# The two halves of a feed-forward tile in a there-and-back order: first-second in one pass, second-first in the next

## The chip, the cores and the metric

The kernel runs on one core of one Trainium2 chip. The metric is the device time of one execution in microseconds (us), which is that of the one core; it is lower when better.

## The reference, cut to what matters

The reference is a two-layer encoder trunk for one sequence of 512 frames with 16 meta tokens ahead of them, 528 positions in all, at a model width of 1024. Each layer is wrapped by two half-step feed-forward blocks, so there are four of them, and between them stand a convolution and state-space mixer (layer 0) and a sliding-window attention (layer 1). A feed-forward block is

```
h = h + 0.5 * (silu(x @ w_gate) * (x @ w_up)) @ w_down      # x = rmsnorm(h)
# x: 528 x 1024, w_gate and w_up: 1024 x 2816, w_down: 2816 x 1024
```

All is in float32. The meta tokens are dropped in the last layer, so the last feed-forward block has 512 positions only.

## The kernel before

**Tiles and passes.** Activations lie with the features on the 128 partitions and the 528 positions as columns. Each product is made at near float32 accuracy from operands that are split into a high and a low part (`xh` and `xl`, `act_h` and `act_l` for activations, `wh` and `wl` for weights, in a reduced float32 format). A tile of 128 output features is the sum over blocks `k` of 128 input features, and for each block over three passes `q`: `wh` with the high part, `wh` with the low part, `wl` with the high part. Weights are the stationary operand and activations the moving one.

**Two halves, two banks.** A matmul result fits into one bank of PSUM, 512 columns. The 528 positions are therefore taken as two halves of 264 columns, `hf` 0 and 1, each accumulated in a bank of its own: a tile has a pair of neighbouring banks, `ps[:, 2 * pair]` for columns 0 to 263 and `ps[:, 2 * pair + 1]` for columns 264 to 527. Each matmul instruction comes with a weight load of its own, so that a weight block that both halves use is loaded twice. In the last feed-forward block there are 512 columns, one half only (`nb` is 1), and every matmul of a tile writes the same bank.

**The helper.** `mm3` (L795) writes all matmuls of a job, one tile's accumulation, in the order k, q, hf; its matmul instruction is L807. `x_job` calls it for gate and up tiles (8 blocks, so 24 passes a job), and `down` inside `ffn` calls it for down tiles, with 12 blocks in the first part of the feed-forward width and 10 in the second (36 and 30 passes). The first two jobs of the first block have copies of this loop in `first_job` (L864) and `second_job` (L879); the mixer's products are at L1048, L1062 and L1090. All of these alternate the halves too, and the change does not touch them.

**Order of the work.** Each engine has its program written out by hand, and the engines wait for each other by semaphores. TensorE (PE) waits for the split weights (`wl_ready`), for the bank pair to be read out (`tile_evac`), and before a job's last block for the activations (`x_ready`, `act_ready`, in `before_last`). The last matmul of a job raises `tile_full`, for which VectorE (DVE) waits before it reads both halves of the pair in one instruction (L1653 and L1656 for gate and up, L1636 for down). Bank pairs 0 and 1 alternate from job to job. SyncE starts the weight transfers, ScalarE (ACT) makes `wh` (L1309), and DVE makes `wl` (L1591).

**Other matmuls that the prediction speaks of.** The sums of squares (`token_sums`, L817) are plain float32 matmuls of 264 columns, and so are those of the state-space part at L1008 and L1009, of 128 columns. A plain float32 matmul shows as two records in the trace, that is two passes over the same columns of the same bank. L1008 and L1009 add up in the same 128 columns, so four records in a row write the same place.

Of the kernel before, what the change touches and what calls it, by code (L numbers as in the profile page):

```python
# [32 lines left out]
def trunk_program(nc, a, out, stop=None):  # L33
# [56 lines left out]
    with ExitStack() as ctx:  # L90
# [706 lines left out]
        def _(pe):  # L797
            def mm3(pair, slot, blocks, x_h, x_l, k0, col, before_last=None, n_last=1):

                c0, nh, nb = col  # L800
                n = len(blocks)
                for k, b in enumerate(blocks):
                    if k == n - n_last and before_last:
                        before_last()
                    for q, (w, x) in enumerate(((wh, x_h), (wh, x_l), (wl, x_h))):
                        for hf in range(nb):
                            last = nc.tensor.matmul(ps[:, 2 * pair + hf, 0:nh], w[:, slot, b * P:(b + 1) * P],  # L807
                                                    x[:, k0 + k, c0 + hf * nh:c0 + (hf + 1) * nh],
                                                    start=(k == 0 and q == 0), stop=(k == n - 1 and q == 2))
                return last  # L810
# [9 lines left out]
            def x_job(u, j, pair, slot, blocks, col, m=None, new_unit=True):  # L820

                if new_unit:
                    pe.wait_ge(wl_ready, u + 1)
                wait(pe, tile_evac, j - 1)
                before = None
                if m is not None:
                    pe.wait_ge(x_ready, KD * m + KD - 1)
                    before = lambda: pe.wait_ge(x_ready, KD * m + KD)
                mm3(pair, slot, blocks, xh, xl, 0, operand(col), before).then_inc(tile_full, 1)
# [53 lines left out]
            def ffn(n, col):  # L883
# [3 lines left out]
                for part, nf in enumerate(PART):  # L887
# [21 lines left out]
                    def down(i):  # L909
                        for s in range(2):  # L910
                            pe.wait_ge(wl_ready, u0 + s + 2 * i + 1)
                            pe.wait_ge(tile_evac, j0 + s + 2 * i - 1)
                            pe.wait_ge(act_ready[n], done - 1)
                            mm3(s, (u0 + s) % 2, range(nf), act_h, act_l, 0, operand(col),
                                lambda: pe.wait_ge(act_ready[n], done)).then_inc(tile_full, 1)
                            if n == 3 and part == 1 and 2 * i + s:
                                output_tile(2 * i + s - 1)
# [1217 lines left out]
```

## Time and profile before

| | |
|---|---|
| time, median of 3 runs | 1878.01 us (1877.99 to 1879.36) |
| profiled execution, own time | 1878.34 us |
| its span, first to last instruction | 1876.5 us |
| granted TensorE clock, mean over the span | 0.999 |
| PE busy, of the span | 99% (13919 matmuls) |
| weight loads (PEld) busy | 94% (13919 loads) |
| DVE, ACT, POOL busy | 51%, 32%, 19% |

The profile is of one execution. A matmul's end is modelled and matmuls overlap, so a busy share of 99% does not say how fast they follow each other; the distance from start to start does, and the chain of work that ended last gives it as a time for so many matmuls. A granted clock of 1.00 is 2.4 GHz, the upper of the engine's two levels.

### The profile page before, as it was taken

What the parts mean: (1) busy time and instruction counts of PE and PEld (TensorE: products, weight loads), DVE (VectorE), ACT (ScalarE), POOL (GpSimd) and SP (SyncE); (2) the same over time, 40 slices, a digit from 0 to 9 for tenths busy, and PEclk for the clock granted to TensorE, in tenths of its full rate; (3) what the DMA queues carried; (4) which work ended last, traced back from release to release, by engine and by line L of the source; (5) the groups of instructions that cost most, each with busy time, mean ns of one, the idle gap of its engine ahead of it and who ended that gap; (6) DMA issues with size and microseconds to landing.
All of it is one profiled execution on the core that took longest, in us unless ns stands there. A gap on an engine that the chain in (4) does not pass through costs nothing.

```text
span 1876.5 us, 33932 instructions
## 1 busy us (share of the span) xinstructions
PE 1867.1 (99%) x13919; PEld 1767.1 (94%) x13919; DVE 959.9 (51%) x1083; ACT 598.4 (32%) x702; POOL 350.1 (19%) x629
## 2 busy tenths in 40 slices
PE   9999999999999999999999999999999999999999
PEld 8999999999999999999999999999988788888887
DVE  6443356668865443344564443445557654434443
ACT  5222222332243222222342222223456442222232
POOL 2888889315230000000000000000012000000000
PEclk9999999999999999999999999999999999999999
DMA  6322544447423332332243223322321233333322
GB/s 184 90 84 84 155 135 130 162 140 191 118 73 89 94 89 86 110 90 73 71 126 90 84 84 101 90 81 80 115 62 46 66 93 94 90 96 101 111 70 87
DMA packets 330785, 188.29 MB, mean 100 GB/s; under 512 B 8152, under 2 KB 323832, under 8 KB 330712
## 3 DMA queue, kind: packets, MB, share of 16 engines
q1 hardware_dynamic: 323216, 166.71, 30.0%
q0 software_dynamic: 7088, 20.38, 3.9%
q8 instruction: 52, 0.85, 0.2%
q10 hardware_dynamic: 408, 0.17, 0.0%
q14 instruction: 21, 0.17, 0.0%
HBM read 174.91 MB, written 11.14 MB: 99 GB/s over the span
## 4 chain that ended last, share of the span: by engine, by line
PE 96%; DVE 2%; issue 1%; ACT 1%; POOL 0%; POOLq 0%; DVEq 0%
PE ps L807 79%; PE ps L1048 5%; PE ps L1159 2%; PE ps L1090 2%; PE ps L1109 1%; PE ps L1298 1%; PE ps L1260 1%; PE ps L1200 0%; PE ps L1009 0%; PE ps L1008 0%; PE ps L999 0%; DVE r L1621 0%; PE ps L1221 0%; PE ps L1211 0%; ACT xh L1321 0%
## 5 line engine op out<-in xcount | busy, mean ns | idle before, releaser
L807 PE MATMUL ps<-xh,wh 128*128 128x264 f32 (+1 forms) x2432 | 557.7, 299 | 0.3 <-DVE t_a L1653 0.2
L807 PE MATMUL ps<-xh,wl 128*128 128x264 f32 (+1 forms) x2432 | 556.6, 299 | 0.0
L807 PE MATMUL ps<-xl,wh 128*128 128x264 f32 (+1 forms) x2432 | 556.6, 299 | 0.0
L1591 DVE TENSOR_TENSOR wl<-raw,wh 128x2048 fp32r<-128x2048 f32 x171 | 400.2, 2340 | 168.4 <-ACT wh L1309 168.4
L1309 ACT ACTIVATE wh<-raw 128x2048 fp32r<-128x2048 f32 x172 | 327.6, 1905 | 246.4 <-PE ps L807 205.5
L807 PEld LDWEIGHTS ps<-xh,wh 128*128 128x128 f32 x2432 | 385.4, 188 | 15.1 <-issue 1.5
L807 PEld LDWEIGHTS ps<-xl,wh 128*128 128x128 f32 x2432 | 385.2, 188 | 13.8 <-issue 0.2
L807 PEld LDWEIGHTS ps<-xh,wl 128*128 128x128 f32 x2432 | 385.2, 188 | 13.8
L807 PE MATMUL ps<-act_h,wh 128*128 128x264 f32 (+1 forms) x1232 | 282.2, 299 | 0.0
L807 PE MATMUL ps<-act_h,wl 128*128 128x264 f32 (+1 forms) x1232 | 281.7, 299 | 0.0
L807 PE MATMUL ps<-act_l,wh 128*128 128x264 f32 (+1 forms) x1232 | 281.6, 298 | 0.0
L1656 DVE TENSOR_TENSOR t_c<-ps,r 128x528 f32<-128x528 f32 (+1 forms) x88 | 62.0, 704 | 355.3 <-PE ps L807 353.2
L807 PEld LDWEIGHTS ps<-act_h,wl 128*128 128x128 f32 x1232 | 195.2, 188 | 7.0
L807 PEld LDWEIGHTS ps<-act_h,wh 128*128 128x128 f32 x1232 | 195.2, 188 | 6.7
L807 PEld LDWEIGHTS ps<-act_l,wh 128*128 128x128 f32 x1232 | 195.2, 188 | 6.7
L1349 ACT ACTIVATE act_h<-t_c 128x528 f32 (+3 forms) x88 | 56.5, 642 | 446.4 <-DVE t_c L1659 446.4
L332 POOL TENSOR_TENSOR arena<-arena 128x32 f32<-128x32 f32 (+6 forms) x253 | 182.6, 722 | 19.6
L682 POOL TENSOR_SCALAR arena<-arena 128x16 f32<-128x16 f32 x4 | 1.0, 257 | 872.5 <-DVE arena L1992 843.3
L1347 ACT ACTIVATE t_bs<-t_a 128x528 f32<-128x528 f32 (+1 forms) x88 | 56.5, 642 | 276.1 <-DVE t_a L1653 276.1
L1636 DVE SCALAR_TENSOR_TENSOR h<-ps,h 128x528 f32 (+2 forms) x71 | 50.0, 704 | 175.9 <-PE ps L807 168.8
L1661 DVE TENSOR_TENSOR act_l<-t_c,act_h 128x528 f32 (+3 forms) x88 | 65.9, 749 | 78.5 <-ACT act_h L1349 78.5
L1659 DVE TENSOR_TENSOR t_c<-t_c,t_bs 128x528 f32<-128x528 f32 (+1 forms) x88 | 69.5, 790 | 9.0
(313 smaller groups left out, 1685.9 us busy)
## 6 DMA issues: line engine op xcount, KB each, us to landing
raw<-in_ff_w_gate SPq DMA_DIRECT2D x88, 512.0 KB, 3.7
raw<-in_ff_w_up SPq DMA_DIRECT2D x87, 512.0 KB, 4.7
raw<-in_ff_w_down SPq DMA_DIRECT2D x64, 384.0 KB, 3.8
raw<-in_ff_w_down SPq DMA_DIRECT2D x64, 320.0 KB, 3.5
raw<-in_even_w_in SPq DMA_DIRECT2D x16, 512.0 KB, 4.8
raw<-in_attn_w_qkv SPq DMA_DIRECT2D x12, 512.0 KB, 4.5
raw<-in_even_w_out SPq DMA_DIRECT2D x8, 512.0 KB, 4.3
raw<-in_attn_w_o SPq DMA_DIRECT2D x8, 512.0 KB, 4.4
```

What stands on the lines that cost most here:

```text
L332: did(g.tensor_tensor(o, x, y, op))
L807: last = nc.tensor.matmul(ps[:, 2 * pair + hf, 0:nh], w[:, slot, b * P:(b + 1) * P], x[:, k0 + k, c0 + hf * nh:c0 + (hf + 1) * nh], start= ...
L1048: last = nc.tensor.matmul(ps[:, 2 * (p % 2) + hf, 0:L // 2], w[:, slot, b * P:(b + 1) * P], x[:, k, hf * L // 2:(hf + 1) * L // 2], start= ...
L1090: last = nc.tensor.matmul(ps[:, 2 * (d % 2) + hf, 0:L // 2], w[:, slot, b * P:(b + 1) * P], x[:, k, hf * L // 2:(hf + 1) * L // 2], start= ...
L1309: nc.scalar.activation(wh[:, c % 2, :], raw[:, c % 2, :], ACT.Copy).then_inc(wh_ready, 1)
L1347: nc.scalar.activation(t_b[:, cols], t_a[:, cols], ACT.Silu).then_inc(silu_done[n], 1)
L1349: nc.scalar.activation(act_h[:, s + 2 * i, span(operand(col))], t_c[:, cols], ACT.Copy).then_inc(act_h_done[n], 1)
L1591: v.tensor_tensor(wl[:, c % 2, :], raw[:, c % 2, :], wh[:, c % 2, :].bitcast(F32), ALU.subtract).then_inc(wl_ready, 1)
L1636: v.scalar_tensor_tensor(hd, tile(pair, col), scale, hd, ALU.mult, ALU.add).then_inc(tile_evac, 1)
L1656: v.tensor_tensor(halves(t_c, col), tile(1, col), halves(r, col), ALU.mult).then_inc(tile_evac, 1)
L1659: v.tensor_tensor(t_c[:, cols], t_c[:, cols], t_b[:, cols], ALU.mult).then_inc(gated[n], 1)
L1661: v.tensor_tensor(act_l[:, s + 2 * i, span(operand(col))], t_c[:, cols], act_h[:, s + 2 * i, span(operand(col))].bitcast(F32), ALU.subtrac ...
```

## The change

One line in `mm3`. The loop over the halves runs forward in the first pass, backward in the second, forward in the third, and so on through the job: the direction is set by whether `3 * k + q`, the number of the pass, is even. With A for the matmul on columns 0 to 263 and B for that on columns 264 to 527, a job was A B, A B, A B, A B and is now A B, B A, A B, B A. The blocks, passes, weights and waits keep their order, and the order of additions within each half is what it was. Since each job has an even number of passes, each now ends with A. With one half only (`nb` is 1) nothing changes.

```diff
                     for q, (w, x) in enumerate(((wh, x_h), (wh, x_l), (wl, x_h))):
-                        for hf in range(nb):
+                        for hf in range(nb) if (3 * k + q) % 2 == 0 else reversed(range(nb)):
                             last = nc.tensor.matmul(ps[:, 2 * pair + hf, 0:nh], w[:, slot, b * P:(b + 1) * P],
                                                     x[:, k0 + k, c0 + hf * nh:c0 + (hf + 1) * nh],
                                                     start=(k == 0 and q == 0), stop=(k == n - 1 and q == 2))
```

The program of PE, at the end of the last up tile of the first feed-forward block's first part and at the start of its first down tile, in the kernel before. A row is a line, an operation, its tiles and its columns; x2 are the two halves of a pass, and a half that waits for a semaphore stands alone.

```order
L807 MATMUL ps<-xl,wh 128x264 x2
L807 MATMUL ps<-xh,wl 128x264 x2
L904 REGISTER_ALU
L904 COMPARE_AND_BRANCH
L807 MATMUL ps<-act_h,wh 128x264 [waits act_ready0,tile_evac]
L807 MATMUL ps<-act_h,wh 128x264
L807 MATMUL ps<-act_l,wh 128x264 x2
L807 MATMUL ps<-act_h,wl 128x264 x2
```

In the changed kernel these rows read the same, since a row does not tell one half from the other; what moved is inside the x2: in every second one the columns from 264 on come first. The comparison of the two programs on PE, on DVE, which reads the tiles, and on the other three engines:

```order
## PE: 3781 rows in the other, 3781 in this; the same
## DVE: 810 rows in the other, 810 in this; the same
## ACT: 492 rows in the other, 492 in this; the same
## POOL: 381 rows in the other, 381 in this; the same
## SP: 275 rows in the other, 275 in this; the same
```

No instruction is added, taken away, or moved to another pass, and no wait moves.

## Rows read from the trace of the kernel before

**Rows 1.** The page: busy times, granted clock by slices, chain by engine and line.
```profile
PE 1867.1 (99%) x13919; PEld 1767.1 (94%) x13919; DVE 959.9 (51%) x1083; ACT 598.4 (32%) x702; POOL 350.1 (19%) x629
...
PEclk9999999999999999999999999999999999999999
...
PE 96%; DVE 2%; issue 1%; ACT 1%; POOL 0%; POOLq 0%; DVEq 0%
PE ps L807 79%; PE ps L1048 5%; PE ps L1159 2%; PE ps L1090 2%; PE ps L1109 1%; PE ps L1298 1%; PE ps L1260 1%; PE ps L1200 0%; PE ps L1009 0%; PE ps L1008 0%; PE ps L999 0%; DVE r L1621 0%; PE ps L1221 0%; PE ps L1211 0%; ACT xh L1321 0%
```

**Rows 2.** The chain in order of time: start us, length us, what; longest pieces.
```profile
41.16 357.12 PE ps L807 x2976
...
589.87 374.65 PE ps L807 x3120
...
971.21 368.89 PE ps L807 x3072
...
1520.65 307.65 PE ps L807 x1356
```

**Rows 3.** Groups of PE by line and shape: count, busy us, mean ns, idle before.
```profile
L807 PE MATMUL ps<-xh,wh 128*128 128x264 f32 x2080 | 420.1, 283 | 0.1
...
L807 PE MATMUL ps<-act_h,wh 128*128 128x264 f32 x1056 | 213.0, 283 | 0.0
...
L807 PE MATMUL ps<-xh,wh 128*128 128x512 f32 x352 | 137.6, 391 | 0.2 <-DVE t_a L1653 0.2
```

**Rows 4.** Stretches, instructions of L807 alone: busy us, granted clock, DMA share.
```profile
620.00:740.00 120.00, 120.00 (x1002) 120.00 (x1002) 1.00 0.29 86
1180.00:1300.00 120.00, 120.00 (x1003) 120.00 (x1002) 1.00 0.27 80
1720.00:1810.00 90.00, 90.00 (x399) 74.59 (x398) 1.00 0.29 85
```

**Rows 5.** Timeline near 156 us, up tile to down tile: start us, length us.
```profile
155.72 0.40 PE L807 MATMUL ps<-xl,wh 128*128 128x264 f32 x2
155.84 0.31 PEld L807 LDWEIGHTS ps<-xh,wl 128*128 128x128 f32 x2
155.96 0.40 PE L807 MATMUL ps<-xh,wl 128*128 128x264 f32 x2
156.09 0.31 PEld L807 LDWEIGHTS ps<-act_h,wh 128*128 128x128 f32 x2
...
156.20 0.40 PE L807 MATMUL ps<-act_h,wh 128*128 128x264 f32 x2
...
156.40 0.71 DVE L1656 TENSOR_TENSOR t_c<-ps,r 128x528 f32<-128x528 f32 x1 [4.45 <-PE ps L807]
156.44 0.40 PE L807 MATMUL ps<-act_l,wh 128*128 128x264 f32 x2
```

**Rows 6.** Timeline of PE near 1640 us, last block, one half of 512 columns.
```profile
1639.74 0.39 PE L807 MATMUL ps<-xh,wh 128*128 128x512 f32 x1
1639.97 0.39 PE L807 MATMUL ps<-xl,wh 128*128 128x512 f32 x1
1640.19 0.39 PE L807 MATMUL ps<-xh,wl 128*128 128x512 f32 x1
1640.42 0.39 PE L807 MATMUL ps<-act_h,wh 128*128 128x512 f32 x1
1640.65 0.39 PE L807 MATMUL ps<-act_l,wh 128*128 128x512 f32 x1
```

**Rows 7.** Timeline of PE near 438 us, plain float32 passes of 128 columns.
```profile
438.07 0.38 PE L1008 MATMUL ps<-arena 128*66 128x128 f32 x2
438.29 0.38 PE L1009 MATMUL ps<-arena 128*66 128x128 f32 x2
...
439.82 0.38 PE L1008 MATMUL ps<-arena 128*66 128x128 f32 x2
```

**Rows 8.** Timeline of PE near 404 us, plain float32 passes of 264 columns.
```profile
403.88 1.05 PE L817 MATMUL ps<-ssq,ones 128*128 128x264 f32 x4
404.58 0.60 PE L1048 MATMUL ps<-xh,wh 128*128 128x264 f32 x2
405.01 0.40 PE L1048 MATMUL ps<-xl,wh 128*128 128x264 f32 x2
```

**Rows 9.** What PE waited for at L807: us in total, times, longest.
```profile
PE ps L807 <- DVE t_a L1653: 0.2, 1, 0.2
```

## The prediction

> **What bounds the kernel now.** I read the page first. The chain that ended last is 96% TensorE, and 79% of the span is the one matmul line that the change edits; the clock stands at its upper level in every slice [rows 1]. Next I looked for waits that the new order could fill or lengthen, and there are none: at L807 TensorE waited 0.2 us in the whole run [rows 9]. So the kernel's time is a count of matmuls times the distance from one start to the next, and this distance is the only thing that the change can move.
>
> The chain in order of time gives it. In the blocks with two halves, 3120 matmuls take 374.65 us, 120.1 ns each, and 3072 take 368.89 us, also 120.1; the first block has 2976 in 357.12 us, 120.0. In the last block, with 512 columns, 1356 take 307.65 us, 226.9 ns each [rows 2]. The stretches say the same (1002 in 120 us), with the clock at 1.00 and the weight loads busy without a gap where the matmuls have 264 columns, but only 74.59 of 90 us where they have 512 [rows 4]. The timeline shows the beat: a pass of two halves every 0.24 us, straight across the end of a tile (155.72, 155.96, 156.20, 156.44), with VectorE reading the finished pair behind it [rows 5].
>
> **The change part by part.** *What is removed, added and moved.* Nothing but the order of the two halves in every second pass. The count of matmuls and of loads stays, and so do all waits: the wait ahead of a job's last block stands before whichever half comes first, and the signal that the tile is full stays on the job's last matmul, when both halves are complete as before. VectorE reads both halves in one instruction, which starts some 0.4 us after the start of the last pass [rows 5]; which half was last is nothing to it. Weight loads do not get fewer: the two halves of a pass have the same weights now, and yet there are 13919 loads for 13919 matmuls [rows 1]. Four in a row with the same `wh` (first and second pass) exist already, and each is loaded. This part of the edit costs nothing, and it needs no cover, since nothing is issued more.
>
> *What differs physically.* Before, every matmul in a tile wrote another bank than the one ahead of it. Now the second matmul of a pass and the first of the next write the same bank, and the same columns of it. How many such places: 2080 matmuls of `xh` and `wh` at 16 a job are 130 gate and up jobs, of 24 passes; 1056 of `act_h` and `wh` are 48 down jobs [rows 3]. All passes together are 1.5 times 3136, so 4704. Less one for each of the 178 jobs, whose end still changes the pair, 4526 places turn from a change of bank into a repeat. With a cost of c ns at each, the time moves by 4.526 us per ns.
>
> *The price c.* No row before shows a repeat with 264 columns of this format, so I bound it from rows nearby.
>
> From above, by the last block. There every matmul repeats its bank within a tile. If a column takes a cycle at 2.4 GHz, as plain passes at two cycles a column suggest (below), 512 columns take 213.3 ns and 264 take 110.0; what is left is 13.6 ns with the bank repeated and 10.1 ns with the bank changed. If the whole difference were the price of repeating, c would be 3.5 ns. That is the upper end: 15.8 us.
>
> From the other side, a change of bank could be what costs, so that c is negative. Of the 10.1 ns that remain with 264 columns, plain passes keep some 2 to 3 (below); the rest, 7 ns at most, would go at each repeat: 31.7 us gained. But the form with no change of bank has the larger remainder, not the smaller.
>
> In the middle, the plain float32 passes. At L1008 and L1009 four records in a row write the same 128 columns of one bank, and from 438.07 to 439.82 us there are 16 records, 109.4 ns each [rows 7]. At L817 two records go to one bank and two to the next; from 403.88 to 405.01 stand these four and one pass of 0.24 us, so 0.89 us for four, 222.5 ns each [rows 8]. The difference is 113.1 ns for 136 columns, 0.83 ns or two cycles a column, and the remainder is 2.7 ns with all repeats (109.4 less 106.7) and 2.5 ns with half of them changes of bank (222.5 less 220.0). Repeating costs no more than changing here, although the same place is written again after 109 ns, sooner than the 120 ns of the changed order. The last block agrees as far as its times are given: from the last up tile to the first down tile the bank changes, and the starts are 0.23 us apart there (1640.19, 1640.42) as between the repeats around it (0.23, 0.22) [rows 6]; at 10 ns a step this excludes a large price, not 3.5 ns.
>
> I take c as zero, by the plain passes, which are nearest to the question asked (a repeat of the same columns after about the same time), while the 3.5 ns rest on two widths that may differ for another reason, for example a cost that grows with the columns.
>
> *The sum.* The profiled execution takes 1878.34 us, of which 1876.5 are span. Plus 4526 times 0 ns this stays 1878.3, and in terms of the median, which lies 0.3 us lower, 1878.0. What a measurement of this kernel can tell from no change is about 0.2%, 3.8 us, or c of 0.83 ns.
>
> **The rivals.** *Repeats cost (slower).* The accumulating write to a bank would have to let the write ahead of it finish, at the pass boundaries of L807. Price up to 3.5 ns at 4526 places, so up to 1893.8 us; from 0.83 ns on it decides. For it: the larger remainder of the 512-column form. Against it: rows 7. The order also makes the moving operand jump back, where second halves used to follow their first halves in memory; if that costs, it has the same sign and place, and I count it here.
>
> *Changes of bank cost (faster).* Then 4526 of them vanish, at up to 7 ns: down to 1846.6 us. For it: the 10.1 ns that no row explains. Against it: the 512-column form and L817, which gain nothing where the bank repeats. The Trainium skill has a rule of this kind (TensorE: Matmul & The Clock Gate, section "A second HAM failure mode: psum-queue depth-cycling"): cycling through PSUM banks at each iteration lets the engine idle so often that its clock is cut back and restored by turns. By that rule fewer changes of bank would speed this kernel up; but the trace shows no cut to undo, since the granted clock is 1.00 in the very stretches that alternate banks at each matmul [rows 4].
>
> *Loads bound it, so no order matters (no change).* Where matmuls have 264 columns, loads lie end to end or over each other for all of 240 us [rows 4]. If it is they that set the beat, a small c would hide behind them: 1878.0 again. This is the forecast by another road. Against it: a transfer that is always under way need not be the one that is waited for.
>
> **How the numbers follow.** No change: 0.76, with a range of its own of 1874.3 to 1881.8. Slower by a repeat's cost: 0.13, spread from 1881.8 to 1893.8. Faster: 0.11, spread from 1846.6 to 1874.3, most of it near the upper end, since all of the 7 ns can hardly go. The range from 1873 to 1888 holds the first case, half of the second and a little of the third, some 0.83 together; the upper end is c of 2.2 ns, beyond the middle of its bounds. The chances by 0.2% are those of the cases.
>
> **What would show it.** If I am right, the chain has pieces of L807 with the same 120.0 to 120.1 ns each (3120 in 374 to 375.4 us), passes 0.24 us apart, weight loads without gaps, and 226.9 ns in the last block. If repeats cost, the 264-column pieces grow, at 3.5 ns to 121.8 ns a matmul (380 us for 3120), and weight loads show gaps at pass boundaries, while the last block stays at 307.65 us. If changes of bank cost, the same pieces shrink. A change in the clock, or a wait of TensorE at L807 above a few us, would mean that something moved which I hold fixed. The prediction is wrong if the start-to-start distance depends on which half went before, which no row of before can show.

## The result, and the profile after

The changed kernel takes 1884.10 us (median of 5 runs, 1881.80 to 1887.51) against 1878.21 us before: a ratio of 1.0031, with a 95% interval of 1.0017 to 1.0045. It is slower by 5.9 us. The forecast was 1878.0 us and no change; the time lies inside the stated range (1873 to 1888), on the side of the rival that I gave 0.13. Measured once more beside the experiments, the same program took 1889.41 us (1884.70 to 1892.58) against 1878.56, a ratio of 1.0057 (1.0044 to 1.0070). So its times scatter over more than 10 us, where those of the kernel before stay within 4. One execution of the kernel before (2235.17 us) and one of the second-first run below (3087.40 us) stand far apart from all others and enter no ratio and no scatter given here.

The page of the changed kernel, its lines that answer to [rows 1]: busy times and the granted clock by slices.

```profile
span 1882.1 us, 33932 instructions
...
PE 1872.2 (99%) x13919; PEld 1771.6 (94%) x13919; DVE 960.1 (51%) x1083; ACT 598.3 (32%) x702; POOL 350.7 (19%) x629
...
PEclk9999999999999999999999999999999999999999
```

Counts, clock and the other engines are as before. The chain in order of time (start us, length us, what), against [rows 2]:

```profile
40.80 280.34 PE ps L807 x2304
...
333.48 70.35 PE ps L807 x576
...
595.43 374.65 PE ps L807 x3120
...
976.77 368.88 PE ps L807 x3072
...
1526.25 307.65 PE ps L807 x1356
```

Read it from the end. The last block has 307.65 us for 1356, to the digit what it had; the second and third blocks have 374.65 and 368.88 us, also the old numbers within 0.01. The first block is the one that changed: 280.34 us for 2304 are 121.7 ns each, where it had 120.0. It begins at 40.80 us (before 41.16) and the next piece after it, the first matmul of the mixer, stands at 403.83 us, where it stood at 41.16 plus 357.12, so at 398.28. The first block is 5.9 us longer, and that is the whole loss: 2976 matmuls times 1.67 ns are 5.0 us, and what TensorE waited at L807, against [rows 9], is another 0.7:

```profile
PE ps L807 <- DVE t_a L1653: 0.9, 2, 0.7
```

Counts of matmuls in a stretch of each of the three blocks with two halves show the pace best (stretch us, its length, PE busy and count, granted clock, DMA share, GB/s). A stretch counts the two matmuls at its edges too, so the pace is the length over the count less two.

```profile
100.00:280.00 180.00, 180.00 (x1482) 1.00 0.37 114
640.00:880.00 240.00, 240.00 (x2002) 1.00 0.31 90
1020.00:1260.00 240.00, 240.00 (x2002) 1.00 0.31 92
```

At 120.0 ns a stretch of 180 us would have 1502, and one of 240 us 2002. The first block has 1482: 121.6 ns, with TensorE busy throughout and the clock at 1.00. In the timeline of the first block (start us, length us) ten starts of passes show it as 2.19 us for nine passes, 0.243 us each, where [rows 5] have 0.24:

```profile
99.77 0.41 PE L807 MATMUL ps<-xh,wh 128*128 128x264 f32 x2
100.01 0.41 PE L807 MATMUL ps<-xl,wh 128*128 128x264 f32 x2
...
101.72 0.40 PE L807 MATMUL ps<-xh,wl 128*128 128x264 f32 x2
101.96 0.28 PE L807 MATMUL ps<-xh,wh 128*128 128x264 f32 x1
```

So one program runs the same loop at two paces, and keeps one for hundreds of microseconds. It does not even begin the block at the longer one. Ahead of the long piece the chain has the block's first two jobs at L807, and then other matmuls:

```profile
28.02 11.52 PE ps L807 x96
...
39.78 1.02 PE ps L977 x8
```

96 matmuls in 11.52 us are 120.0 ns each; the longer pace starts behind the break. The starts in the kept trace, read to the nanosecond, show what it is made of. From 100 to 150 us the distances come round every 12 matmuls (125, 124, 123, 118, 125, 121, 120, 124, 120, 116, 124, 120; together 1460 ns, 121.67 each), from 640 to 700 us every four (119, 121, 120, 120). In the longer pace the distances are 120.5 ns on the mean at the boundary of two passes, where a half is repeated, and 122.8 inside a pass: the added time does not stand at the repeat.

### The profile page after: what moved, and what is told of

It is laid out like the page before. It is cut to its first block, busy times and chain, and to the rows that moved or that the text cites. A ratio compares the mean times of both kernels' runs of the same rounds, so it can differ in the third digit from the quotient of the medians.

```text
span 1882.1 us, 33932 instructions
## 1 busy us (share of the span) xinstructions
PE 1872.2 (99%) x13919; PEld 1771.6 (94%) x13919; DVE 960.1 (51%) x1083; ACT 598.3 (32%) x702; POOL 350.7 (19%) x629
## 4 chain that ended last, share of the span: by engine, by line
PE 95%; DVE 2%; issue 1%; ACT 1%; DMA 0%; POOL 0%; SPq 0%; ACTq 0%; DVEq 0%
PE ps L807 78%; PE ps L1048 5%; PE ps L1159 2%; PE ps L1090 2%; PE ps L1109 1%; PE ps L1298 1%; PE ps L1260 1%; PE ps L1200 0%; DMA raw<-in_ff_w_gate 0%; PE ps L1009 0%; PE ps L1008 0%; PE ps L999 0%; DVE r L1621 0%; PE ps L1221 0%; PE ps L879 0%
## 5 line engine op out<-in xcount | busy, mean ns | idle before, releaser
L807 PE MATMUL ps<-xh,wh 128*128 128x264 f32 (+1 forms) x2432 | 558.5, 299 | 0.9 <-DVE t_a L1653 0.9
L807 PE MATMUL ps<-xl,wh 128*128 128x264 f32 (+1 forms) x2432 | 557.0, 299 | 0.0
L807 PE MATMUL ps<-xh,wl 128*128 128x264 f32 (+1 forms) x2432 | 555.7, 298 | 0.0
L807 PEld LDWEIGHTS ps<-xh,wh 128*128 128x128 f32 x2432 | 385.7, 188 | 16.0 <-issue 1.4
L807 PEld LDWEIGHTS ps<-xh,wl 128*128 128x128 f32 x2432 | 386.5, 188 | 13.9
L807 PEld LDWEIGHTS ps<-xl,wh 128*128 128x128 f32 x2432 | 386.6, 188 | 13.8 <-issue 0.2
L807 PE MATMUL ps<-act_h,wh 128*128 128x264 f32 (+1 forms) x1232 | 282.5, 299 | 0.0
L807 PE MATMUL ps<-act_l,wh 128*128 128x264 f32 (+1 forms) x1232 | 281.8, 299 | 0.0
L807 PE MATMUL ps<-act_h,wl 128*128 128x264 f32 (+1 forms) x1232 | 281.2, 298 | 0.0
L807 PEld LDWEIGHTS ps<-act_h,wl 128*128 128x128 f32 x1232 | 195.8, 188 | 7.1
L807 PEld LDWEIGHTS ps<-act_l,wh 128*128 128x128 f32 x1232 | 195.8, 188 | 6.6
L807 PEld LDWEIGHTS ps<-act_h,wh 128*128 128x128 f32 x1232 | 195.3, 188 | 6.8
L332 POOL TENSOR_TENSOR arena<-arena 128x32 f32<-128x32 f32 (+6 forms) x253 | 192.4, 760 | 19.6
```

The lines of the kernel that those rows point to most:

```text
L332: did(g.tensor_tensor(o, x, y, op))
```

## The experiments

All are timed beside the kernel before on the same chip. In what follows A is the matmul on columns 0 to 263, B that on 264 to 527. "Pace" is that of the three stretches above, in ns a matmul. The diffs of banks and columns alone are against the changed kernel; the others hold for the kernel before, or for the changed kernel where the order A B B A is named. Where a diff sets `at`, the moving columns are read from `at` on; that line is left out in the last ones.

### The changed kernel again

> The changed kernel once more, as the measure for the others on the same chip. In its profile above, the first block ran at 121.7 ns a matmul and the second and third at 120.1. Theory S (a block falls into one of two states at its start and keeps it; in the one state the new order costs 1.67 ns a matmul, in the other nothing): times scatter from about 1878 to 1893.5 us in steps of some 5 us a block (3000 matmuls times 1.67 ns), and each block of the profile is either at 120.0 to 120.1 or at about 121.7 ns. Rival F (a fixed cost of the first block, say of its transfers): 1884 us in every run within 1 us, first block slow, the other two not.

1889.41 us (1884.70 to 1892.58), 1.0057 (1.0044 to 1.0070). Stretches in this profile, and the chain around the start of its second block:

```profile
100.00:280.00 180.00, 180.00 (x1482) 1.00 0.37 114
640.00:880.00 240.00, 240.00 (x2003) 1.00 0.31 91
1020.00:1260.00 240.00, 240.00 (x2002) 1.00 0.31 92
```
```profile
583.71 5.84 PE ps L807 x48
589.55 0.89 PE ps L817 x4
590.44 21.64 PE ps L807 x178
```

Again the first block is at 121.6 and the others are at 120.0, but the second block began at the other pace: its first job took 5.84 us for 48 (121.7 ns; before the change 5.76 to 5.77). By 640 us it ran at 120.0. In between, the stream was broken by the sums of squares (L817) at 589.55 us, and by a gap at 596.24 us, where the timeline has a pass that begins 0.36 us after the one ahead of it. So a block does not keep the pace that it begins with, as theory S had it. The scatter fits the rest of theory S: one block at the longer pace costs about 5.2 us, two 10.4, three 15.6, so that 1884, 1889 and 1893 are such sums. The profiled executions agree: 1884.10 and 1884.70 us with one long block, 1889.20 with two (columns alone, below). Some times (1887.5, 1881.8) lie between, as they would if a block changed its pace on the way; none of these has a trace. Rival F, a fixed cost of the first block, falls by the scatter and by the run with turned columns alone, below.

### The banks alone, and the columns alone

```diff
-for hf in range(nb) if (3 * k + q) % 2 == 0 else reversed(range(nb)):
-    matmul(ps[:, 2 * pair + hf, ...], ..., x[..., c0 + hf * nh:...])
+for hf in range(nb):                       # banks only
+    bank = hf if (3 * k + q) % 2 == 0 else nb - 1 - hf
+    matmul(ps[:, 2 * pair + bank, ...], ..., x[..., c0 + hf * nh:...])
...
+for hf in range(nb):                       # columns only
+    half = hf if (3 * k + q) % 2 == 0 else nb - 1 - hf
+    matmul(ps[:, 2 * pair + hf, ...], ..., x[..., c0 + half * nh:...])
```

> Columns are read first-second in every pass as before; only the bank written goes there and back, so the halves' sums are mixed (the output is not the reference's). It has the 4526 repeats of a bank without the jump in the moving columns. Theory B (the repeat of a bank is what costs, in the bad state): 1880 to 1888 us, with blocks at 121.7 ns. Theory M (the order of the moving columns is what costs): every block at 120.0 to 120.1 ns, 1877 to 1879 us.

> Columns are read there and back, the banks are written first-second in every pass, so the halves' sums are mixed (the output is not the reference's). It has the changed order of the moving columns and no repeat of a bank. Theory M: 1880 to 1888 us, with blocks at 121.7 ns. Theory B: every block at 120.0 to 120.1 ns, 1877 to 1879 us.

Banks only: 1879.28 us, 1.0002 (0.9993 to 1.0010). Columns only: 1889.82 us, 1.0058 (1.0041 to 1.0075). The stretches of banks only, then of columns only:

```profile
100.00:280.00 180.00, 180.00 (x1502) 1.00 0.37 114
640.00:880.00 240.00, 240.00 (x2002) 1.00 0.31 90
1020.00:1260.00 240.00, 240.00 (x2002) 1.00 0.31 90
```
```profile
100.00:280.00 180.00, 180.00 (x1482) 1.00 0.37 114
640.00:880.00 240.00, 240.00 (x2002) 1.00 0.31 90
1020.00:1260.00 240.00, 240.00 (x1975) 1.00 0.31 92
```

Theory B is out. With all its 4526 repeats of a bank the kernel is as fast as before, and with no repeat of a bank, but with the columns turned, it has the changed kernel's loss and its two paces, here in the first and the third block (1975 is 121.6 ns). The third block takes the longer pace between its first job behind the sums of squares and the next:

```profile
971.10 5.76 PE ps L808 x48
976.90 373.99 PE ps L808 x3072
```

That is 120.0 ns, then 121.7; the second block of the run above went the other way at the same place.

### The second half moved

```diff
-x[:, k0 + k, c0 + hf * nh:c0 + (hf + 1) * nh]
+at = c0 + hf * 256       # A B B A; later A B A B.  In a third run: c0 + hf * 248, A B B A
+x[:, k0 + k, at:at + nh]
```

> The changed order, but the second half of a tile reads columns 256 to 519 instead of 264 to 527 (8 columns are taken twice and the last 8 left out, so the output is not the reference's): it starts at a multiple of 64 bytes in its row, as the first half does, and not in the middle of such a piece. Theory M in the form that the place of the second half in memory decides: no block above 120.1 ns, 1877 to 1879 us. Theory B, or M in the form that any change of order costs: as the changed kernel, blocks at 121.7 ns, 1880 to 1888 us.

> The order of the kernel before, first-second in every pass, with the second half at columns 256 to 519 (8 columns twice, the last 8 left out). No matmul begins at the column of the one ahead of it, but all begin at a multiple of 64 bytes. Theory R and theory O: 120.0 to 120.1 ns, 1878 us. Theory P: 121.7 ns in every block, 1893 us, as with the changed order.

> The changed order with the second half at columns 248 to 511 (16 columns twice, the last 16 left out): it begins in the middle of a 64-byte piece as at 264, but no longer where the first half ends. Theory P: as the changed kernel, each block at 120.1 or at 121.7 ns, 1878 to 1894 us with scatter. Theory R: the same. A theory in which the second half has to follow the first in memory: another pace, in all blocks, as with the second half at 256.

A B B A with 256: 1893.84 us, 1.0079 (1.0066 to 1.0092), 121.6 ns in all three blocks. My expectation that it would cure the loss was wrong: it made the longer pace permanent, and the times lie within 2 us. A B A B with 256 is worse still, 1910.15 us, 1.0168 (1.0151 to 1.0185), though its order is that of the kernel before:

```profile
100.00:280.00 180.00, 180.00 (x1462) 1.00 0.37 112
640.00:880.00 240.00, 240.00 (x1948) 1.00 0.30 88
1020.00:1260.00 240.00, 240.00 (x1948) 1.00 0.30 88
```

That is 123.3 ns in every block; 3.3 ns on 9408 matmuls are 31 us, nearly the whole difference of 31.8. So a loss of this kind needs no turned halves at all. Theory R (to begin at the column of the matmul ahead costs) and theory O (the order A B B A itself costs) as put there fall; theory P (to begin at the same place within 16 columns costs) foretold a loss, but 121.7 ns. With the second half at 248 (A B B A): 1882.50 us, 1.0018 (1.0009 to 1.0028), 120.4 ns in all blocks (1497, 1996, 1996), neither of the two paces that P and R expected. The third theory of this run, that the second half has to follow the first in memory, allowed another pace in all blocks; the cut at 272 and the run with alternating places, both below, speak against it.

### One half twice

```diff
-x[:, k0 + k, c0 + hf * nh:c0 + (hf + 1) * nh]
+at = c0                  # first half twice; second half twice: c0 + (nb - 1) * nh
+x[:, k0 + k, at:at + nh]
```

> Forward order and banks as in the kernel before, but both matmuls of a pass read columns 0 to 263 (the second half of the positions is left out, so the output is not the reference's): every matmul begins at the same column as the one ahead of it. Theory R (beginning at the same column as the matmul ahead costs 3.33 ns in the bad state, 0 in the good one; twice 1.67): blocks at 120.1 or at 123.3 ns a matmul, 1878 to 1909 us. Theory P (what counts is whether the beginnings change place within a 64-byte piece: 0 and half a piece in turn is free, the same place again is not; with the second half at column 256 all beginnings were at place 0 and every block was at 121.7): every block at 121.7 ns, 1893 us, without scatter. Theory O (the order A B B A itself, whatever the columns): 120.1 ns, 1878 us.

> As the run with the first half twice, but both matmuls of a pass read columns 264 to 527 (the first half is left out): all beginnings lie in the middle of a 64-byte piece. Theory R: blocks at 120.1 or 123.3 ns, 1878 to 1909 us. Theory P: the same pace as with the first half twice if only the change of place counts, another if place 0 and the middle differ by themselves. Theory O: 1878 us.

First half twice: 1883.78 us, 1.0033 (1.0023 to 1.0043). Second half twice: 1899.37 us, 1.0108 (1.0091 to 1.0125), 122.2 ns in all blocks (1475, 1966, 1966). The stretches with the first half twice:

```profile
100.00:280.00 180.00, 180.00 (x1502) 1.00 0.37 113
640.00:880.00 240.00, 240.00 (x2002) 1.00 0.31 90
1020.00:1260.00 240.00, 240.00 (x1981) 1.00 0.30 88
```

120.0, 120.0 and 121.3 ns: two paces again, with another upper one. The second block began at the other pace here too, and left it behind the break. None of R, P and O gives these numbers. Beginning always at the same place can be free (first half) or not (second half).

### Turning once per block, going backward always, another cut

```diff
-for hf in range(nb):
+for hf in range(nb) if k % 2 == 0 else reversed(range(nb)):        # turned once per block
...
+for hf in reversed(range(nb)):                                     # second-first in each pass
...
+at, n_c = c0 + hf * 272, (272, 256)[hf] if nb > 1 else nh          # cut at 272
```

> The order of the halves turns once per block of 128 inputs instead of once per pass (A B A B A B, B A B A B A), so a job has 7 repeats of a half where the changed kernel has 23. Theory R (each repeat has a price of its own, 3.33 ns in the bad state): bad blocks at 120.5 ns a matmul, good ones at 120.0, 1878 to 1883 us. Rival Q (the pace belongs to the whole repeating sequence, not to the single repeat): another pace, not 120.5, or no loss at all.

> Second-first in every pass (B A B A): the moving columns go back in each pass, no half is repeated. Theory R and Q: 120.0 to 120.1 ns in every block, 1878 us, no scatter. Rival (going back within a pass is what costs): blocks at 121.7 ns or more, 1884 us or more.

> First-second in every pass, but the tile is cut at column 272 instead of 264: halves of 272 and 256 columns, each beginning at a multiple of 64 bytes, 528 columns in all as before (VectorE still reads 264 of each bank, so the output is not the reference's). If the place of the second half's beginning sets the pace, as with 256: about 123.3 ns a matmul, 1909 us. If the cut at 256 was slow because its two halves overlap: 120.0 ns, 1878 us. If whole pieces save reads: under 120 ns, under 1878 us.

Turned once per block: 1888.59 us, 1.0053 (1.0037 to 1.0070), 121.1 ns in all blocks (1488, 1984, 1984). With a third of the repeats it loses as much as the changed kernel, in every block, where a price per repeat gives 120.5 at most: the pace belongs to the sequence. Second-first: 1879.31 us, 1.0003 (0.9993 to 1.0013), 120.0 ns (1503, 2003, 2002): going backward is free. Cut at 272: 1908.95 us, 1.0162 (1.0145 to 1.0179), 123.3 ns (1462, 1949, 1949), as with 256, though here the halves do not overlap and the second follows the first. Halves that both begin at a multiple of 16 columns are the slow ones in this order.

### The weight blocks moved

```diff
-w[:, slot, b * P:(b + 1) * P]
+wc = b * P if nb == 1 else b * P + 8 if b < BLK - 1 else b * P - 8
+w[:, slot, wc:wc + P]        # together with at = c0 + hf * 256, A B A B
```

> The run with first-second order and the second half at 256 (123.3 ns in every block, 1910 us), with one thing more: each weight block is read 8 columns further on (the last of a unit 8 columns back), so that weight loads begin in the middle of a 64-byte piece (weights are mixed and the output is not the reference's). Theory W (the reads of weights and of moving columns get in each other's way, and their places decide): another pace than 123.3 ns. Theory V (the moving columns alone set the pace): 123.3 ns again, 1910 us.

1902.71 us, 1.0127 (1.0110 to 1.0144), against 1.0168 with the weights in their place.

```profile
100.00:280.00 180.00, 180.00 (x1475) 1.00 0.37 114
640.00:880.00 240.00, 240.00 (x1957) 1.00 0.31 91
1020.00:1260.00 240.00, 240.00 (x1957) 1.00 0.31 92
```

122.2 ns in the first block and 122.8 in the others instead of 123.3, and nothing was moved but the columns from which weights are loaded. These are means of two paces. Stretches of down tiles alone, in the first and in the second block, show them:

```profile
165.00:225.00 60.00, 60.00 (x496) 1.00 0.41 128
735.00:795.00 60.00, 60.00 (x489) 1.00 0.34 101
```

That is 121.5 and 123.2 ns; with the weights in their place the first of these stretches has 489 too. This is theory W: the places of the loads have a part in the pace. How the two reads meet, and why the down tiles gain in one block and not in the other, is not shown by it.

### Turned halves with alternating places, and the wide block

```diff
+odd = (3 * k + q) % 2
-for hf in range(nb):
+for hf in reversed(range(nb)) if odd else range(nb):
+    at = c0 + hf * nh + ((-8 if hf else 8) * odd if nb > 1 else 0)     # first run
...
+    at = c0 + hf * nh + (8 * odd if nb == 1 else 0)                    # second run, forward order
```

> The changed order A B B A, but in the backward passes the second half is read from column 256 and the first from column 8 (8 columns off, so the output is not the reference's): the halves turn as in the changed kernel, while beginnings at a multiple of 64 bytes and beginnings in the middle of such a piece alternate from matmul to matmul as in the kernel before. Theory A (strict alternation of the two places is what keeps the pace at 120.0 ns): every block at 120.0 to 120.1 ns, 1878 us, no scatter. Rival H (the halves' own order or the distance in columns decides): blocks at 121.7 ns at least in part, 1882 us or more, with scatter or above 1885 in all runs.

> The kernel before, but in the last feed-forward block (one half of 512 columns) every second matmul reads 8 columns further on (the output is not the reference's), so that the two places alternate there too; the blocks with two halves are as before. Theory A carried to this width: under 226.7 ns a matmul in the last block, by up to 3.3 ns, since 226.7 is 34 times 6.67 ns (16 columns) and 223.3 is 33.5 times: down to 1873 us. Rival (alternation helps only where halves begin or end within a piece by their width): 226.7 ns or more, 1878 us or more.

The first is the deciding run. The halves turn as in the changed kernel and their banks repeat as there, but beginnings at a multiple of 16 columns (0, 256) and 8 columns past one (264, 8) alternate from matmul to matmul as in the kernel before:

```profile
100.00:280.00 180.00, 180.00 (x1502) 1.00 0.37 114
640.00:880.00 240.00, 240.00 (x2002) 1.00 0.31 90
1020.00:1260.00 240.00, 240.00 (x2003) 1.00 0.31 90
```

120.0 ns in all blocks, 1878.50 us, 0.9997 (0.9987 to 1.0007), 10 runs from 1877.08 to 1880.27: the loss and the scatter are gone. This is what theory A foretold, and rival H falls as put. The run also takes away something else: no matmul here begins at the very column of the one ahead of it. That the place within 16 columns does not decide alone is said by the run with 248, whose places follow each other as in the changed kernel, at 120.4 ns. Theory A does not carry to 512 columns, where the same alternation costs: 1883.21 us, 1.0025 (1.0015 to 1.0034), and the chain's piece of the last block, against the 307.65 us of [rows 2], is

```profile
1521.24 312.12 PE ps L809 x1356
```

or 230.2 ns a matmul instead of 226.9.

## Why the prediction was wrong

**What bounds the kernel** held. Nothing but the distance of starts moved: no long wait, no clock, no other engine, and 5.0 of the 5.9 us in the profile are matmul pace. The other part, a wait of 0.7 us in the first block, is for a bank pair to be read out (DVE t_a L1653). The two other traces of turned columns with a long first block (the changed kernel again, columns alone) have it too; the kernel before has not, nor has A B B A with 256, whose first block is as slow. What brings it was not isolated.

**What is removed, added and moved** held: the same 13919 loads and matmuls, the same waits.

**What differs physically** is the step that failed. I wrote that the new order turns a change of bank into a repeat, and priced that. The bank has no part in it (1.0002 with all the repeats); the order of the moving columns alone makes the loss (1.0058, with 121.7 instead of 120.0 ns a matmul in the blocks that take the longer pace). What differs is where each matmul's moving columns begin after those of the one ahead of it. The kernel before alternates 0 and 264, a multiple of 16 columns and 8 past one; A B B A gives the sequence 0, 264, 264, 0. I mentioned that the moving operand jumps back and let it ride with the bank, as something of the "same sign and place", without a price of its own. The last sentence of the prediction names what came true, a distance that depends on which half went before, but no term of the sum stood for it.

**The price c** was then read from the wrong rows. The plain float32 passes [rows 7] answer for the bank and rightly give zero. They say nothing on moving columns of this format. The upper bound of 3.5 ns, from the remainders of the two widths, came close in size: c of 3.5 was to give 121.8 ns, and the bad pace is 121.6 to 121.7. But that it is a price at each repeat is refuted by turning once per block (7 repeats a job, 121.1 ns, where the price would give 120.5), by the forward order with 256, which repeats no half and runs at 123.3, and by the distances in the slow stretch, which are longer inside the passes (122.8 ns) than at the repeats (120.5). The agreement in size is no support for it.

**The rivals.** "Repeats cost" had the sign, the line and the size, and as a mechanism it was half wrong: the bank, its main clause, costs nothing, and the moving columns, its side clause, do. The sign that it named, gaps in the weight loads, did not come (below). "Changes of bank cost" is refuted by the banks-only run from the other side, since 4526 fewer changes gained nothing. The Trainium skill's rule named there, on banks in turn and the clock (TensorE: Matmul & The Clock Gate, "A second HAM failure mode: psum-queue depth-cycling"), has no case here: the clock is 1.00 in every stretch above, whatever the banks do. "Loads bound it, so no order matters" is refuted as put, since loads lie end to end at 120.0 ns [rows 4], at 121.7 and at 123.3 alike. The first line is of the changed kernel's first block, the second of the forward order with 256; behind the length stand busy time and count of TensorE, then of the loads:

```profile
100.00:280.00 180.00, 180.00 (x1482) 180.00 (x1481) 1.00 0.37 114
620.00:740.00 120.00, 120.00 (x975) 120.00 (x975) 1.00 0.28 81
```

But loads do take part, as the run with moved weight blocks shows. On this the Trainium skill says (TensorE: Matmul & The Clock Gate, section "Step-by-step: what each phase is for") that weights and moving columns are read through two independent ports, so that a load takes no read bandwidth from the running matmul. Read as saying that the two do not touch each other, this would have moving the weight blocks change nothing; it changed 1.0168 to 1.0127, and 123.3 to 122.8 ns on the mean of a block. The measurement decides: the two are not independent here.

**What is shown and what stays open.** Shown: bank order is free; column order alone makes the loss; in each of the four orders in which the two places alternate strictly (the kernel before, banks only, second-first, and turned halves with alternating places) the pace is 120.0 ns; without turning, the loss appears when both halves begin at multiples of 16 columns; a block of the changed kernel runs at 120.0 or 121.7 ns, and in the kept traces leaves one pace for the other where the stream was broken. Not shown: what in the chip makes places matter, why a block takes the one pace or the other, and why the first half taken twice, with no alternation at all, ran two blocks at 120.0. Alternation was enough for the pace in these runs, not needed for it, and the result at 248 (120.4) says that a multiple of 16 is not the whole rule. None of the versions tried beats the kernel before.

## What to carry to other kernels

When a kernel is bound by the distance between matmul starts, the order and the starting columns of the moving operand are part of its tuning, even if no instruction and no wait changes: here 8 columns decide 1.7%. Price a reordering by everything that changes from one instruction to the next, one by one (bank, moving columns, weights), and look for a row that varies exactly that; a row that varies something else gives a clean zero for the wrong question. If one program's times scatter while its neighbour's do not, compare the pace of the same loop in its stretches before looking for a cause that is the same in each run.

## What the runs showed of the hardware that was not expected

The pace of back-to-back 264-column matmuls took the values 120.0, 120.4, 121.1, 121.3, 121.7, 122.2 and 123.3 ns at a granted clock of 1.00, with TensorE and the weight loads busy without a gap in each case. 16 cycles of 2.4 GHz take 6.67 ns; 120.0 is 18 of these, 121.7 is 18.25 and 123.3 is 18.5, but 120.4, 121.1, 121.3 and 122.2 fall between, so that the paces show no single step. This is arithmetic on the paces, not a cause that was isolated.

One program, with the same data, can run a block of 3000 matmuls at either of two paces for more than 200 us and end up to 11 us apart from run to run. The kernel before has one pace only in its trace, which fits times that agree within 4 us.
